# A retrieval of expert rows in which every sixteenth gather is issued as two gathers of complementary experts

## The reference

```python
sub_scores = einsum('thcd,hckd->thck', q, sub_keys)          # 8 heads, 2 sets of 128 keys
vals, ids = top_k(sub_scores, 16)
cand = vals[:, :, 0, :, None] + vals[:, :, 1, None, :]
top_sc, pos = top_k(cand.reshape(t, 8, 256), 16)
eid = i1 * 128 + i2                                          # 16 of 16384 experts for each head
gate = softmax(top_sc)
u = u_tab[eb]                                                # 2048 values a row
act = gelu(einsum('td,tkd->tk', xb, u))
out = einsum('tk,tkd->td', gb * act, v_tab[eb])              # 2048 values a row
```

## Time and profile before

| | us |
|---|---|
| runs of the kernel before | 3300.18, 3301.16 |
| median | 3300.67 |
| profiled execution, first to last instruction (span) | 3298.4 |
| first gather issued, from the span's start | 1993.78 |
| last gather issued, from the span's start | 3264.03 |

### The profile page before, as it was taken

One profiled execution on the slowest core, in us unless ns is written; L12 is line 12 of the kernel. 1 busy time (PEld: TensorE's weight loads), 2 busy tenths in 40 slices (PEclk: granted clock), 3 DMA queues, 4 the chain that ended last, 5 costly groups with the idle time before them and its releaser, 6 DMA issues.

```text
span 3298.4 us, 43218 instructions
## 1 busy us (share of the span) xinstructions
PE 3018.7 (92%) x17823; PEld 2359.9 (72%) x17823; DVE 1922.1 (58%) x2901; ACT 1283.0 (39%) x2358; POOL 358.4 (11%) x357
## 2 busy tenths in 40 slices
PE   7999999999999999999999999888888877777777
PEld 7889879999999999989999997444444333232332
DVE  5567675555545555677765554555555665555654
ACT  5555554444434345665544342222222222222222
POOL 0000000000000001100000012222123222222221
PEclk9999999999999999999999999999999989999999
DMA  8554446555555555554455348999999999999998
GB/s 254 182 198 154 155 151 221 184 185 179 185 186 179 183 188 192 186 171 150 154 191 203 130 156 378 430 431 430 431 430 431 431 425 431 430 432 430 431 431 355
DMA packets 95204, 913.14 MB, mean 277 GB/s; under 512 B 10580, under 2 KB 15068, under 8 KB 20000
## 3 DMA queue, kind: packets, MB, share of 16 engines
q0 software_dynamic: 38896, 543.71, 38.7%
q1 hardware_dynamic: 48672, 346.38, 30.1%
q10 hardware_dynamic: 7440, 20.29, 2.0%
HBM read 900.89 MB, written 9.45 MB: 276 GB/s over the span
## 4 chain that ended last, share of the span: by engine, by line
PE 65%; DMA 23%; DVE 7%; ACT 4%; issue 1%; SPq 0%; ACTq 0%; POOL 0%; DVEq 0%; POOLq 0%
PE sums L573 15%; PE sums L574 14%; PE sums L575 14%; DMA area<-in_uv,cst 12%; PE sums L1057 10%; DMA ringx<-in_uv,cst 7%; DMA ring<-in_uv,cst 2%; PE sums L1014 2%; DVE area L2390 2%; PE sums L637 1%; PE sums L639 1%; PE sums L638 1%; DVE wl L1769 1%; ACT cst L1110 1%; DVE ringx L2390 1%
## 5 line engine op out<-in xcount | busy, mean ns | idle before, releaser
L1769 DVE TENSOR_TENSOR wl<-ring,wh 128x1024 fp32r<-128x1024 f32 x612 | 749.2, 1229 | 586.8 <-ACT wh L1110 586.1
L1110 ACT ACTIVATE wh<-ring 128x1024 fp32r<-128x1024 f32 x612 | 643.4, 1054 | 442.9 <-PE sums L575 391.9
L1110 ACT ACTIVATE cst<-cst 128x1 f32<-128x1 f32 (+2 forms) x787 | 234.9, 299 | 914.8 <-DVE cst L2390 853.2
L1057 PE MATMUL sums<-area,cst 128*128 128x512 f32 x1032 | 481.3, 613 | 99.6 <-ACT cst L1110 99.5
L1057 PEld LDWEIGHTS sums<-area,cst 128*128 128x128 f32 x1032 | 193.4, 194 | 367.9 <-issue 200.5
L2390 DVE CUSTOM_DVE_ANT_0 area<-area 128x2048 f32<-128x2048 f32 x129 | 295.5, 2291 | 268.8 <-DMA area<-in_uv,cst 268.8
L573 PE MATMUL sums<-normed,wh 128*128 128x256 f32 x1440 | 407.3, 283 | 0.0
L575 PE MATMUL sums<-normed,wl 128*128 128x256 f32 x1440 | 406.9, 283 | 0.0
L1057 PE MATMUL sums<-ringx,cst 128*128 128x512 f32 x680 | 317.0, 611 | 88.6 <-ACT cst L1110 88.6
L1057 PEld LDWEIGHTS sums<-ringx,cst 128*128 128x128 f32 x680 | 126.6, 193 | 266.6 <-ACT cst L1110 135.5
L2390 DVE CUSTOM_DVE_ANT_0 ringx<-ringx,area 128x2048 f32<-128x2048 f32 x86 | 197.1, 2291 | 183.7 <-DMA ringx<-in_uv,cst 183.6
(11 more groups left out here) (371 smaller groups left out, 5635.6 us busy)
## 6 DMA issues: line engine op xcount, KB each, us to landing
ring<-in_w_in_a SPq DMA_DIRECT2D x66, 1024.0 KB, 4.9
ring<-in_w_up SPq DMA_DIRECT2D x64, 1024.0 KB, 4.8
ring<-in_w_down SPq DMA_DIRECT2D x64, 1024.0 KB, 4.9
ring<-in_w_out SPq DMA_DIRECT2D x32, 1024.0 KB, 5.0
ring<-in_w_in_b SPq DMA_DIRECT2D x16, 1024.0 KB, 4.9
ring<-in_w_xk SPq DMA_DIRECT2D x16, 1024.0 KB, 5.2
ring<-in_w_xv SPq DMA_DIRECT2D x16, 1024.0 KB, 5.2
ring<-in_w_xq SPq DMA_DIRECT2D x16, 1024.0 KB, 4.9
```

Of the source, the lines that this page charges most:

```text
L1057: mm = te.matmul(sums[t][:, 512 * i:512 * i + 512], diag[:, n % 2, :], v[:, 512 * i:512 * i + 512], start=False, stop=n % 128 == 127)
L1110: return sc.activation(out, in_, f, **kw)
L1769: ve.tensor_tensor(wl[:, j % 3, :], ring[:, load % 3, j % 2 * 1024:j % 2 * 1024 + 1024], wh[:, j % 3, :], ALU.subtract).then_inc(lo_in, 1)
```

## The change

Sixteen of the 256 gathers, n = 9, 25, 41 and so on to 249, are issued as two. `topk(g)` computes, beside `eid`, two index columns `apart` for expert number 9 of its head: in the first every index below 8192 has 16384 added, in the second every index of 8192 or more. Each gather has a bound of 16383 on the index and leaves a row out whose index is beyond it, so each token's row comes with exactly one of the two, into the same buffer. Between the two GpSimd waits for the first to have landed. The counts of landed gathers (`NTH`) go up by two at such an n.

```diff
+        apart = sr(2, 16).bitcast(I32)
...
+        APART = [n % 16 == 9 for n in range(256)]
-        NTH = [sum(BUF[m] == BUF[n] for m in range(n + 1)) for n in range(256)]
+        NTH = [sum(1 + APART[m] for m in range(n + 1) if BUF[m] == BUF[n]) for n in range(256)]
...
(in topk, ahead of the write of eid)
+                x = eq[:, 0, 0:3]
+                own(ve.scalar_tensor_tensor(x[:, 0:1], sel[:, 0, 9:10], 128.0, sel[:, 1, 9:10], ALU.mult, ALU.add))
+                on.wait_ge(v_seq, seq.n)
+                own(ve.tensor_scalar(x[:, 1:2], x[:, 0:1], 8192.0, 16384.0, ALU.is_lt, ALU.mult))
+                own(ve.tensor_scalar(x[:, 2:3], x[:, 0:1], 8192.0, 16384.0, ALU.is_ge, ALU.mult))
+                on.wait_ge(v_seq, seq.n)
+                for a in range(2):
+                    own(ve.tensor_tensor(apart[:, a, g:g + 1], x[:, 0:1], x[:, 1 + a:2 + a], ALU.add))
+                on.wait_ge(v_seq, seq.n)
...
(in gpsimd, for gather n)
-                if n < 255:
+                if APART[n]:
+                    for a in range(2):
+                        gp.indirect_dma_start(rowbuf[BUF[n]], None, A["uv"], which(apart[:, a, n // 16:n // 16 + 1]),
+                                              bounds_check=16383, oob_is_err=False).then_inc(rows_in[BUF[n]], 16)
+                        if a == 0:
+                            on.wait_ge(rows_in[BUF[n]], 16 * (NTH[n] - 1))
+                elif n < 255:
```

## The result

The changed kernel takes 3410.02 us (median of two runs, 3408.68 to 3411.36) against 3300.67: ratio 1.0332, interval 1.0315 to 1.0349, so 109 us or 3.3% slower. Forecast were 3385 us in a range of 3340 to 3428, at 0.75 for slower by over 2%. The profiled execution has a span of 3406.9 us, 108.5 us more than before.

A forecast was written before the change was run, and what follows sets the result against it. The prediction took the 16 full DMA engines as the bound: 16 * (2.4 gap + 2.15 random + 0.9 engines' own) = 87 us, less 2.7 of tail, 84 us on 3300.67 gave 3385 us, range 3340 to 3428.

The forecast's parts named there:

- gap only: Rival: at each pair's wait only the 2.4 us gap is lost, engines end evenly; 3339 us, chance 0.20 with cases near it.
- hidden: Rival: buffers' round trip sets the pace and engines catch up after each gap, so time stays 3301 us; chance 0.03.
- The hole: Gap at each pair's wait, from last data of the first gather to first data of the next: 2.4 us.
- the step to GpSimd's start: First part of the gap, last data to GpSimd's next instruction: 0.6 us plus 0.2 for its wake, 0.8 us.
- the step to first data: Second part of the gap, gather issue to first data on idle engines: 1.6 us, 0.94 to 1.0 of it descriptors.
- the queue is full again at once and nothing further is lost: After each wait, gathers follow with 0.94 us of descriptor making against 4.86 us of transfer: no further loss, nothing won back.
- the rival of left-out rows moved after all: Rival: each gather of a pair takes 128 rows' time, left-out rows included; 131 us more, 3431 us, chance 0.09.
- Unevenness: At each wait, engines ending apart: 2.15 us from random row shares plus 0.9 us from engines not being alike.
- the random part: Random split of each engine's 8 rows: the largest of 16 engines lies 3.5 rows, 2.15 us, beyond the even share.
- rule of 128 + k' - k: Rows an engine carries between two waits, k and k' its old and new first-gather rows; variance 4, deviation 2 rows.
- What was costed at nothing: Parts of the change put at 0 us: VectorE's small operations (0.8 at worst), bytes, and the first gather's descriptors.
- The tail: End of the kernel: engines already stop over 2.7 us, mostly reset by the last wait at n = 249, so subtracted.

The follow-up runs named there:

- changed_seven: Changed kernel's order, but only the nine pairs at n = 121 to 249, where there are seven row buffers: 3360.97 us, +60.6 against the kernel before.
- bound_alone: Kernel before, with the index bound on every sixteenth whole gather, leaving no row out, and no wait: 3301.86 us, ratio 1.0004.
- columns_no_wait: Kernel before, with every sixteenth gather issued as two, u half and v half of all 128 rows, no bound, no wait: 3302.65 us, ratio 1.0006.
- parity: Changed kernel, but rows go to first or second gather by their partition's parity, so each engine has 4 of 8 rows in each: 3388.25 us.
- the pair of columns with a wait: Kernel before, every sixteenth gather split into u half and v half of all rows, GpSimd waiting for the first, no bound: 3376.08 us, ratio 1.0229.
- the turned blocks: Changed kernel, but pairs split by partitions 0 to 63 and 64 to 127, the blocks changing places from pair to pair: 3458.24 us, ratio 1.0475.
- later_seven: Changed kernel with only the nine pairs at n = 121 to 249, wait and second gather behind gather n + 2: 3306.54 us, ratio 1.0019.

## Why the prediction was right, and where it was off

The forecast held in kind and in range: the engines are the bound, a wait that empties their queue isn't made up, and the loss stands at the pairs: with no pair before n = 110 (`changed_seven`) the slices there are at 430 GB/s, and with the bound or a second gather but no wait (`bound_alone`, `columns_no_wait`) nothing is lost that can be told. Of the rivals, gap only (3339 us) is ruled out by parity, 49 us above it with even shares, and "hidden" by every run with such a wait. It was 25 us short, in its terms:

- **The hole**: "together 2.4 us". Measured 2.8. The step to GpSimd's start was put at 0.8 and took 1.1 (0.35 + 0.79), of which 0.5 comes with the bound; the step to first data was put at 1.6 and took 1.7. 16 times: 45 us for 38. The reading behind the 0.8 was off: the data does not end at 3282.75. A packet counts where it starts, the window after that is empty by chance, and one engine goes on with its 8 KB rows of the last gathers until 3285.5:

```profile
3283.75:3284.00 0.25, 0.00 (x0) 0.00 (x0) 0.25 (x1) 0.16 (x2) 0.00 (x0) 1.00 0.08 33
```

By the packet records the last u row that the dot at 3283.38 needs ends at 3283.02, so from data to dot it is 0.36 us and not 0.6, as in the hole. Without the bound the step takes 0.35 + 0.27 = 0.6 us, less than the 0.8; the bound, costed at nothing, adds the 0.5.

- **Slow rows after the hole**: not in the sum at all; the prediction had "the queue is full again at once and nothing further is lost". The queue's share times the span is the time that the engines spend on gather packets: 0.387 * 3298.4 = 1276 before, 0.381 * 3406.9 = 1298 after (3 us or so of rounding in the difference), 22 us more for the same rows, 1.3 a pair. The windows show them after the hole. This is the step that was missing, and the largest of the misses. It also settles the rival of left-out rows moved after all: that would be 16 * 4.86 = 78 us more of share; parity, where as many rows are left out, has 0.383 * 3385.9 = 1297, and the pair of columns with a wait, where none is, 0.383 * 3373.4 = 1292.
- **Unevenness**: forecast 3.05 us a pair, 2.15 random and 0.9 the engines' own. The packet records give the idle time of the 16 engines, as a mean: 2.0 us a pair while they run out and 0.4 after the first data, 38 us in all. In parity it is 1.05 and 0.25, so the random part is 1.1 (with 0.3 of slower rows the 1.4 of above) and the rest 1.3. The total was 0.6 too high, the random part put at twice its size and the other too low. Its rule of 128 + k' - k was shown by the turned blocks.
- **What was costed at nothing** was nothing while the queue is full: bound, second gather and VectorE's small operations, with `bound_alone` and `columns_no_wait` (both keep them) at +1 and +2 us. The packets of the rows left out are in neither; at 0.01 us each they are under 0.1 us a pair, and `later_seven`, which has them, loses 1.5 us between its landings.
- **The tail**, taken off at 2.7 us: the same mean idle time in the last 20 us of the gathers is 3.5 us before and 1.1 after, so 2.4 us were won back. The four terms make 45 + 22 + 38 - 2 = 103 us of the 108.5 by which the span grew; 5 us or so are left without an account.

The Trainium skill's figure in "DMA: Bandwidth & Descriptors", Anatomy of one DMA, about 2.0 us of fixed cost for each DMA, gives 32 us for the 16 additional ones. The runs don't bear that out as the cost of a gather: 16 additional gathers without a wait cost 1.7 us (5 at most by the interval), and 16 waits without an additional gather 97. The cost is the wait's, and 2.0 us is short even of the hole, 2.8 us or 2.3 without the bound. Nor is it mostly completion, as the prediction has it from there: 0.35 us lie behind the last data, and 1.64 to 1.70 between GpSimd's start and the first.

Open stays why rows after a hole, or in a short queue, are slow, and whether the rows left out are read from HBM as its counter says.

## What to carry to other kernels

Where the DMA engines are the bound, ask of each wait on the issuing engine what will still be queued when it ends. If nothing, it costs the hole, the slow restart and the engines' unevenness, here 4.7 to 6.8 us each (7.4 and 9.8 with blocks of partitions), whatever the DMA behind it costs itself. Issuing other transfers ahead of the wait hid nearly all of it where there were seven buffers, but the buffer is then held longer, so count whether the ring of buffers comes round later than that (31.7 against 24.3 and 34.0 us here), and whether something at the end still waits for it (5 us here). And if a transfer must be split, split it so that every engine has the same rows between two waits.

## What was not expected of the hardware

- After an empty queue the first row of each engine takes about twice its 0.61 us (1.21 on average; share 1.88 for 393 GB/s in half a microsecond). In the changed kernel the full rate is back some 6 us after the first data; behind a whole gather, where each engine has its 8 rows, only the first rows are slow.
- A gather with a bound on the index starts 0.79 us after the landing that it waits for, one without 0.27 us.
- A row left out makes a packet of 4 bytes; the HBM read counter rises by the row's full 16 KB all the same.
- Descriptors that start within a dot take 2.87 us for 0.94 at every one of 16 waits; the landing releases both at once.
